# Two transformer blocks in one launch: the query root of the first attention on GpSimd, a fused negated minimum, another order at three exits, and interleaved feed-forward begins

## The reference

```
# first block
h = rmsnorm(x); z = h @ w_in                      # pool | u, v | two gates
y_a = pool_mixer(z_pool) @ w_branch_a
y_b = (gelu(u) * (tril(w_spatial) . rmsnorm(gelu(v)) + b_spatial)) @ w_branch_b
x += (sigmoid(g_a) * y_a + sigmoid(g_b) * y_b) @ w_out
x += conv_ffn(rmsnorm(x))                         # up 2 x 2816, 3-tap conv, gelu * b, down
x += sigmoid(rmsnorm(x) @ w_ple_gate) * (p @ w_ple)
x  = rmsnorm(x)
# second block, layer 0: sliding window attention; layer 1: latent attention
x += 0.5 * swiglu(rmsnorm(x)); x += attention(rmsnorm(x)); x += 0.5 * swiglu(rmsnorm(x))

def sliding_window_attention(h, ...):             # 16 heads of 64, 2 key heads, window 128
    q, k, v = split(h @ w_in)
    q, k = rmsnorm(q, q_gain), rmsnorm(k, k_gain) # over the 64 of each head
    scores = q . k / 8 + bias[bucket(distance)]   # blocks of 128 queries x 256 keys
    m = max(max(scores), sink)
    p = exp(scores - m) / (sum(exp(scores - m)) + exp(sink - m))
    return (p . v) @ w_out
```

## Time and profile before

| | |
|---|---|
| median of 3 runs | 2787.8 us (2785.0 to 2788.22) |
| profiled execution, its own time | 2790.39 us |
| its span in the profile | 2789.2 us |
| TensorE busy | 2696.5 us, 97% |
| VectorE, ScalarE, GpSimd busy | 1473.3, 972.5, 315.3 us |
| mean granted TensorE clock | 0.984 |
| chain that ended last | 86% TensorE, 8% VectorE, 4% ScalarE |

### The profile page before, as it was taken

How to read it: one execution, slowest core, us unless ns; L and a number is a source line. 1 busy time by engine, 2 the same in 40 slices (tenths; PEclk the granted TensorE clock), 3 DMA queues, 4 the chain that set the end, 5 groups by cost and what they waited for, 6 DMA issues and landing times.

```text
span 2789.2 us, 32273 instructions
## 1 busy us (share of the span) xinstructions
PE 2696.5 (97%) x13207; PEld 2260.6 (81%) x13207; DVE 1473.3 (53%) x2362; ACT 972.5 (35%) x1602; POOL 315.3 (11%) x389
## 2 busy tenths in 40 slices
PE   6899999999998999999899999999999989999999
PEld 5788788888876888888887888888888878888887
DVE  4635545655567545456675444454343677544433
ACT  3334233333354212124544222232222477432221
POOL 2000000000012000003341000010000387300000
PEclk9999999999999999999899999999999999999999
DMA  4222223623132275737222322233222200232321
GB/s 139 93 98 82 76 91 122 205 89 108 65 102 76 91 106 78 106 105 109 92 72 91 106 91 97 83 108 99 95 93 91 63 31 31 78 104 91 106 87 64
DMA packets 281194, 258.99 MB, mean 93 GB/s; under 512 B 40516, under 2 KB 276055, under 8 KB 281047
## 3 DMA queue, kind: packets, MB, share of 16 engines
q1 hardware_dynamic: 281047, 256.93, 32.0%
HBM read 242.23 MB, written 14.68 MB: 92 GB/s over the span
## 4 chain that ended last, share of the span: by engine, by line
PE 86%; DVE 8%; ACT 4%; issue 1%; POOL 0%; SPq 0%; DMA 0%; DVEq 0%; ACTq 0%; POOLq 0%
PE bank L1070 28%; PE bank L1072 27%; PE bank L1071 27%; DVE Wl L1741 1%; PE bank L1213 1%; PE bank L1081 1%; ACT Wh L1405 1%; DVE TMP L1934 1%; DVE TMP L1931 1%; DVE TMP L1810 1%; ACT TMP L1518 0%; DVE Pl L1729 0%; ACT Hh L1418 0%; PE bank L1264 0%; DVE nt L1714 0%
## 5 line engine op out<-in xcount | busy, mean ns | idle before, releaser
L1070 PE MATMUL bank<-Hh,Wl 128*128 128x512 f32 x2144 | 845.9, 395 | 15.9 <-DVE Hl L1757 15.9
L1071 PE MATMUL bank<-Hl,Wh 128*128 128x512 f32 x2144 | 838.9, 391 | 0.0
L1072 PE MATMUL bank<-Hh,Wh 128*128 128x512 f32 x2144 | 838.7, 391 | 0.0
L1405 ACT ACTIVATE Wh<-RAW 128x1024 fp32r<-128x1024 f32 (+2 forms) x454 | 441.0, 1022 | 431.8 <-PE bank L1072 391.6
L1741 DVE TENSOR_TENSOR Wl<-RAW,Wh 128x1024 fp32r<-128x1024 f32 (+2 forms) x420 | 492.6, 1216 | 170.0 <-ACT Wh L1405 169.5
L1070 PEld LDWEIGHTS bank<-Hh,Wl 128*128 128x128 f32 x2144 | 404.6, 189 | 104.2 <-issue 8.2
L1070 PE MATMUL bank<-Ph,Wl 128*128 128x512 f32 x1200 | 473.5, 395 | 13.2 <-DVE Pl L1823 3.5
L1072 PEld LDWEIGHTS bank<-Hh,Wh 128*128 128x128 f32 x2144 | 404.6, 189 | 86.2
L1071 PEld LDWEIGHTS bank<-Hl,Wh 128*128 128x128 f32 x2144 | 404.9, 189 | 85.6 <-issue 1.7
L1072 PE MATMUL bank<-Ph,Wh 128*128 128x512 f32 x1200 | 469.5, 391 | 0.0
L1071 PE MATMUL bank<-Pl,Wh 128*128 128x512 f32 x1200 | 469.3, 391 | 0.0
(11 more groups left out here) (295 smaller groups left out, 2473.1 us busy)
## 6 DMA issues: line engine op xcount, KB each, us to landing
RAW<-in_ffn_wg SPq DMA_DIRECT2D x44, 1024.0 KB, 5.2
RAW<-in_ffn_wu SPq DMA_DIRECT2D x44, 1024.0 KB, 5.1
RAW<-in_ffn_wd SPq DMA_DIRECT2D x32, 1024.0 KB, 5.2
RAW<-in_w_up SPq DMA_DIRECT2D x22, 1024.0 KB, 5.1
RAW<-in_w_in SPq DMA_DIRECT2D x20, 1024.0 KB, 5.1
RAW<-in_ffn_wd SPq DMA_DIRECT2D x16, 768.0 KB, 4.4
bias_scratch<-M SPq DMA_DIRECT2D x16, 512.0 KB, 8.1
RAW<-in_w_down SPq DMA_DIRECT2D x8, 1024.0 KB, 5.8
```

The costliest lines, as they stand in the source:

```text
L1070: mm(o, ll, rh, start=start, stop=False)
L1071: mm(o, lh, rl, start=False, stop=False)
L1072: return mm(o, lh, rh, start=False, stop=stop)
L1405: run(Wh[:, n % 3, x:y], RAW[:, n % 2, x:y], ACT.Copy).then_inc(*w_hi.up(("w_hi", n, i)))
```

## The change

- `ffn` begins with `dense_wide` for both `a` banks, then a norm step, then the `b` product with one norm step after each bank. The steps of s3's norm move from places 1 and 3 to 0 and 2.
- The first gate tile `gb` 0 is multiplied before `mix(7)`.
- Gate exit: the last `pg` bank tells after each chunk that it has been read (`frees`), and `Hh` of chunk c waits for that alone. The steps are reordered as the diff shows, with halves of chunks 0 to 2 ahead of the sums of chunk 6.
- `out_partial`: halves and sums follow one chunk behind `add_x`.
- First attention: the query root is an add and a power on GpSimd; the factor 1/8 goes into it (64 eps), and so out of the key gain. The scores are kept negated with their negated minimum, from one instruction; the exponential takes scale -1 and starts after the first half of the scores. An extra exponential on one column stands in `a_kv`.

Removed and added lines (a line "..." leaves unchanged ones out):

```diff
@@ -236,7 +236,7 @@
-    def dense(names, n, K, src, vi=0, base=0, kw=0, scaled=False, wide=False, ring=None):
+    def dense(names, n, K, src, vi=0, base=0, kw=0, scaled=False, wide=False, ring=None, frees=None):
@@ -245,7 +245,7 @@
-            do("dense", b, n, vi, K, src, ready, base, kw + c)
+            do("dense", b, n, vi, K, src, ready, base, kw + c, frees)
@@ -337,9 +337,10 @@
-                dense(ba, na, 8, "H", scaled=not begins)
+                dense(ba, na, 8, "H", scaled=not begins, wide=begins)
...
+                    norm_step()
@@ -499,6 +500,7 @@
+    gate_tile("gb", 0)
@@ -507,7 +509,7 @@
-    gated("wb", "gb", 8, branch_b)
+    gated("wb", "gb", 8, branch_b, True)
@@ -544,27 +546,41 @@
-    def gate_x(cc, b):
-        t = tmps.take(("t_pg", cc))
+    def gate_x(cc):
+        b, t = ("pg", cc // 2, cc % 2), tmps.take(("t_pg", cc))
...
+
+    def sums_x(cc):
...
-    for i in range(4):
-        n = next_tile("pg", i, 1 if i == 3 else 2)
+    for i in range(3):
+        n = next_tile("pg", i, 2)
...
-        gate_x(2 * i, ("pg", i, 0))
-        if i == 3:
-            h_new("s0")
-            for c in range(5):
-                h_pair(c, None)
-        gate_x(2 * i + 1, ("pg", i, 1))
-    for c in range(5, 8):
+        for c in range(2):
+            gate_x(2 * i + c)
+            sums_x(2 * i + c)
+    n = next_tile("pg", 3, 1)
+    dense([("pg", 3, 0)], n, 8, "H", scaled=True)
+    gate_x(6)
+    dense([("pg", 3, 1)], n, 8, "H", kw=1, frees="s0")
+    do("used", n)
+    h_new("s0")
+    for c in range(3):
...
+    sums_x(6)
+    h_pair(3, None)
+    scale([("pg", 3, 1)])
+    for c in (4, 5):
+        h_pair(c, None)
+    gate_x(7)
+    for c in (6, 7):
+        h_pair(c, None)
+    sums_x(7)
@@ -598,7 +614,7 @@
-    norm_begin("s3", "RF", (1, 3))
+    norm_begin("s3", "RF", (0, 2))
@@ -615,14 +631,14 @@
-            do("dense", b, held[j], 0, 2, src, keys(), base, c)
+            do("dense", b, held[j], 0, 2, src, keys(), base, c, None)
...
-            if j == 3:
+            for x in [c - 1] * (j == 3 and c > 0) + [c] * (j == 3 and c == 7):
...
-                    after(c)
-                if c < late:
-                    sums(c)
+                    after(x)
+                if x < late:
+                    sums(x)
@@ -924,7 +940,7 @@
-    mhalf, most = sm[:, 11:12], sm[:, 12:13]
+    mhalf, most, eps64 = sm[:, 11:12], sm[:, 12:13], sm[:, 14:15]
@@ -1012,10 +1028,10 @@
-    gk_a8 = sm[:, 10:11]
+    nsink = small[:, 48:64]
...
-    ssq, rq = small[:, 16:32], small[:, 32:48]
+    ssq, rq, rms = small[:, 16:32], small[:, 32:48], small[:, 64:80]
@@ -1112,7 +1128,7 @@
-                b, n, vi, K, src, keys, base, c = s
+                b, n, vi, K, src, keys, base, c, frees = s
@@ -1121,7 +1137,10 @@
-                ins.then_inc(*bank_full.up(b))
+                    if frees:
+                        ins.then_inc(*bank_full.up(("h_read", frees, k), *([b] if k == K - 1 else [])))
+                if not frees:
+                    ins.then_inc(*bank_full.up(b))
@@ -1412,7 +1431,7 @@
-                act.wait_ge(*maybe(("h_read", ver)))
+                act.wait_ge(*maybe(("h_read", ver, c) if ver == "s0" else ("h_read", ver)))
@@ -1559,6 +1578,8 @@
+                if half:
+                    run(sm[:, 13:14], mhalf, ACT.Exp)
@@ -1572,7 +1593,7 @@
-                run(Ph[:, g, :], bank(("a_kt", g)), ACT.Copy, scale=gk_a8).then_inc(*pair_hi.up(("a_kT_hi", g)))
+                run(Ph[:, g, :], bank(("a_kt", g)), ACT.Copy, scale=gk_a).then_inc(*pair_hi.up(("a_kT_hi", g)))
@@ -1584,9 +1605,10 @@
-                act.wait_ge(*at(("a_nmax", h)))
...
-                    run(S[:, z0:z1], S[:, z0:z1], ACT.Exp, bias=nm[:, n:n + 1], accum_out=sums_[:, n:n + 1])
+                    if n % 2 == 0:
+                        act.wait_ge(*at(("a_biased", h, n // 2)))
+                    run(S[:, z0:z1], S[:, z0:z1], ACT.Exp, bias=nm[:, n:n + 1], scale=-1.0, accum_out=sums_[:, n:n + 1])
@@ -2017,8 +2039,7 @@
-                ts(gk_a8, gk_a, 0.125, None, ALU.mult).then_inc(*dve_out.up("a_gain"))
-                dve.wait_ge(*at("a_gain"))
+                ts(nsink, sinkc, -1.0, None, ALU.mult).then_inc(*dve_out.up("a_sinks"))
@@ -2047,12 +2068,12 @@
+                if g and b == 0:
+                    dve.wait_ge(*at(("a_qss_in", g - 1)))
...
-                dve.wait_ge(*at(("a_qss", g, 3)))
-                rsqrt(rq, ssq, 64, ("a_rq", g))
@@ -2060,7 +2081,7 @@
-                stt(Pl[:, g, :], bank(("a_kt", g)), gk_a8, f(Ph[:, g, :]), ALU.mult, ALU.subtract).then_inc(
+                stt(Pl[:, g, :], bank(("a_kt", g)), gk_a, f(Ph[:, g, :]), ALU.mult, ALU.subtract).then_inc(
@@ -2072,7 +2093,8 @@
-                mx, nm = sm[:, 160 + x:164 + x], sm[:, 164 + x:168 + x]
+                nm = sm[:, 164 + x:168 + x]
+                dve.wait_ge(*at("a_sinks"))
@@ -2082,11 +2104,9 @@
-                        ins = dve.e.tensor_tensor_reduce(S[:, z0:z1], o[:, z0 - c0:z1 - c0], B[:, z0:z1], 1.0,
-                                                         sinkc[:, h:h + 1], ALU.add, ALU.max, mx[:, n:n + 1])
+                        ins = dve.e.tensor_tensor_reduce(S[:, z0:z1], o[:, z0 - c0:z1 - c0], B[:, z0:z1], -1.0,
+                                                         nsink[:, h:h + 1], ALU.add, ALU.min, nm[:, n:n + 1])
...
-                dve.wait_ge(*at(("a_biased", h, 1)))
-                ts(nm, mx, -1.0, None, ALU.mult).then_inc(*dve_out.up(("a_nmax", h)))
@@ -2228,6 +2248,7 @@
+                memset(eps64, 64 * EPS)
@@ -2282,6 +2303,16 @@
+            elif kind == "a_q_norm":
+                g, = s
+                pool.wait_ge(*at(("a_qss", g, 3)))
+                if g:
+                    pool.wait_ge(*at(("a_rq", g - 1)))
+                tt(rms, ssq, eps64.broadcast_to([128, 16]), ALU.add).then_inc(*pool_out.up(("a_qss_in", g)))
+                pool.wait_ge(*at(("a_qss_in", g)))
+                if g:
+                    pool.wait_ge(*at(("a_qn", g - 1)))
+                tt(rq, rms, mhalf.broadcast_to([128, 16]), ALU.pow).then_inc(*pool_out.up(("a_rq", g)))
```

## The result

The changed kernel takes 2753.1 us (median of 4 runs, 2752.5 to 2753.7) against 2788.0 us (2785.0 to 2789.4) for the kernel before on the same chip: ratio 0.9876, 95% interval 0.9859 to 0.9893, 34.9 us less. The forecast was 2758 us, 29.3 us less.

The account below looks back on a forecast made before the run. TensorE, busy 97% of the span, was taken as the bound, leaving only idle and low-clock time to win. Terms of 8.2, 4, 6.6, 3 and 7.5 sum to 29.3 us off 2787.8: 2758 us, range 2745 to 2774.

Parts of the forecast that it names:

- Part 1: Gate tile ahead of the last mixing product: 5.3 us of wait plus 2.9 of low clock, 8.2 us gained.
- Part 2: Gate exit into feed-forward s0: the changed order starts TensorE 3.3 us earlier; gain 4 us, bounds 0 and 8.
- Part 3: First attention, query root on GpSimd: 6.6 us from waits and 3 us from the clock.
- the waits for `M`: First attention: TensorE's waits for normalised queries shrink by 6.6 us, with VectorE's multiply held by GpSimd's split.
- The clock: First attention: less time at the low clock behind the waits, 3 us, bounds 0 and 9.5.
- no wait of TensorE goes back to the exponentials, so this is worth nothing: First attention: the fused negation and earlier exponentials gain 0; were their cover gone, 3 us.
- Part 4: First attention's exit and wide begins: 3.0 us of waits plus 4.5 of low clock, 7.5 us gained.
- The other begins: Begins of feed-forwards f, s2 and s3: no wait now, worth 0; uncovered, up to 5.4 us each.
- its sign of error: At `wb` 0, behind the last mixing product: a new TensorE wait on `Pl` would show the forecast wrong.
- GpSimd takes the gain in: Rival: multiply held by both split halves, exits' low halves alternating badly with square sums; 13 us gained, 2775 us, chance 0.10.
- the clock does not come back: Rival: waits shrink but still leave the low clock everywhere; 19 us gained, 2769 us, chance 0.15.
- the third: Rival: nothing is held and the clock stays high; 42 us gained, 2745 us, chance 0.10.

Follow-up runs that it names:

- e1: The kernel before with only the first gate tile moved ahead of the last mixing product: 2780.35 us, ratio 0.9968.
- e3: The kernel before with only the gate exit's new order and marks by row, feed-forwards still begun bank by bank: 2788.12 us, ratio 0.9994.
- e5: The kernel before with only the wide feed-forward begins: 2780.94 us, ratio 0.9970.
- e6: The changed kernel with the feed-forwards begun bank by bank again: 2756.88 us, ratio 0.9885.
- e13: The changed kernel itself, measured again in later rounds: 2756.33 us, ratio 0.9876.
- e7: The changed kernel with a separate negation on VectorE and the exponentials waiting for it, as in the kernel before: 2756.89 us, ratio 0.9885.
- e2: The kernel before with only the query root moved to GpSimd, the separate negation kept: 2776.2 us, ratio 0.9953.
- e12: The changed kernel with later query weight splits, s0's first rows ahead of the gate's seventh addition, and f begun bank by bank: 2755.63 us, ratio 0.9869.
- e10: The changed kernel without ScalarE's small early exponential that brings its table load ahead: 2757.4 us, ratio 0.9879.

## Why the prediction was right, and where it was not

**Part 1** was right in both halves, 8.2 for 8.4 (e1: 8.1 in its trace, 8.9 by the ratio). No wait for `Pl` at `wb` 0 appeared.

**Part 2** was right in its sum, 4 for 3.7, and in the step that mattered: `X` 6 held by a square sum (1.64 us for 0.69), `Hl` 0 behind it, first row 2.7 us late for the 3 forecast. Wrong was the attribution. I gave 4 us to the order and 0 to s0's wide begin; e3 shows that the order alone gives 1.4 at most, e5 the wide begin alone about 1, and the pair gives 3.7. My working had TensorE's matmuls of both banks in it, but not that the column sums between them need all eight rows and the last square sum.

**Part 3** was mis-sized: 9.6 for 14.7. By its terms: the waits for `M` gave 7.8 us (9.2 to 1.4) where 6.6 were forecast, because the third multiply was not held and the second was asked for 1.05 us later, against GpSimd's queue, than worked out. The clock gave 9.5 - 3.4 = 6.1 (the one stretch left has 6.80 us at 0.50) where I took 3 between bounds of 0 and 9.5. And 1.5 us of waits for `Pl` went (2.6 to 1.1), which I had not counted, while those for the query copies grew from 3.0 to 3.4. The size of the clock's part is that of this one trace: the clock was low for 6.8 us behind the first group here and not in e6, and 1.00 behind the second here and low for 3.4 us in e13. The step that failed in kind is "no wait of TensorE goes back to the exponentials, so this is worth nothing". It does, by way of GpSimd's queue, into which the change itself had put the root: e7 shows 1.05 us of wait; its 2.5 us in all are not told from noise. I had listed what is queued behind the root, and not what the root is queued behind once the exponentials move. e2, the root with the old exponentials, gave 12.2. And the stretched instruction of the earlier trace rows (128x16, 2.33 us for 0.17) has one input, so that of the rows I showed only the add of the earlier trace rows spoke for the multiply's being held.

**Part 4** was right, 7.5 for 8.0, and so was the chain: the low halves come every 1.70 us, each held to 1.18 or 1.19 us:

```profile
1436.77 0.68 DVE L1969 SCALAR_TENSOR_TENSOR X<-bank,X 128x512 f32<-128x512 f32 x1
1437.37 1.18 DVE L1779 SCALAR_TENSOR_TENSOR Hl<-X,P,Hh 128x512 fp32r<-128x512 f32 x1
1438.47 0.68 DVE L1969 SCALAR_TENSOR_TENSOR X<-bank,X 128x512 f32<-128x512 f32 x1
```

But either half alone gives 7 of the 8. The other begins were put at 0: f costs 0.6 us, by a wait for `Pl` in f that the forecast had not named (its sign of error was one at `wb` 0):

```profile
522.33 0.50 PE L1086 MATMUL bank<-Ph,Wl 128*128 128x512 f32 x1 [1.00 <-DVE Pl L1751]
```

It was 0.4 us before the change, and is 0.45 and 0.42 in e6 and e12, where f begins bank by bank. That the later scaling pushes the low halves behind it on VectorE is my reading of the order, not tried by itself.

**The rivals.** That GpSimd takes the gain in did not come: the multiply is held by one instruction, never by both. That the clock does not come back holds at the first group, and at s0, where the forecast had counted on nothing from it. Of the third, that nothing is held was wrong and that the clock stays high nearly right, and the time lies between its 2745 and the forecast.

## What to carry to other kernels

When work moves to another engine's queue, follow that queue in both directions: what stands ahead of the moved instruction may hang on something that had been free until then. Two edits that cure one wait don't add, and two that need each other are worth little apart, so a sum over the parts of a change is tried at its places of overlap first. At an exit with eight rows to hand over, look for the instruction that needs the last row: all that is done for the first ones ends there.

## What was not expected of the hardware

One wait, two clocks. At the first group's turn TensorE waits 1.12 us in the changed kernel and 1.12 us in e6, with the same work on all engines around it. In the first the clock is low from 1293.5 to 1300.3; in e6, by windows, it is not low at all, 3.0 us to its favour:

```profile
1290.00:1300.00 10.00, 7.75 (x62) 7.05 (x61) 7.70 (x18) 5.46 (x17) 5.30 (x4) 1.00 0.39 137
1300.00:1312.00 12.00, 11.94 (x95) 11.03 (x93) 8.63 (x23) 8.52 (x26) 9.31 (x7) 1.00 0.31 91
```

So after the same wait the clock fell in one execution and stayed in the other. What decides is open; the size of the clock's part in any one trace, 1.5 to 3 us a place, is to be taken with that doubt.

The wait at the first group changes from one execution to the next, and it follows a weight transfer. GpSimd's split of the second query tile, seen in four executions, begins when ScalarE's high half does, and that when the transfer has landed; in the changed kernel:

```profile
1272.58 2.01 ACT L1424 ACTIVATE Wh<-RAW 128x1024 fp32r<-128x1024 f32 x2 [11.53 <-DMA RAW<-in_a_w_in]
```

```profile
1273.72 4.77 POOL L2272 TENSOR_TENSOR Wl<-RAW,Wh 128x1024 fp32r<-128x1024 f32 x2 [9.16 <-ACT Wh L1424]
```

```profile
1277.21 1.31 DVE L1722 TENSOR_SCALAR nt<-sm 128x8 f32<-128x8 f32 x1
1278.56 0.17 DVE L1730 TENSOR_SCALAR nt<-nt 128x8 int32<-128x8 int32 x1
```

An instruction of VectorE on 8 elements per partition, 0.17 us when free, is held until the split ends at 1278.49, and behind it stand the keys' root, the queries' sums, GpSimd's root and the multiply:

| kernel | split ends | multiply starts | TensorE asks | its wait |
|---|---|---|---|---|
| changed | 1278.49 | 1287.33 | 1289.67 | 1.12 |
| e13 (changed) | 1279.21 | 1287.79 | 1289.38 | 1.85 |
| e10 | 1280.94 | 1289.52 | 1290.50 | 2.45 |
| e12 | 1281.51 | 1290.08 | 1290.96 | 2.55 |

In the last three the multiply starts 8.57 or 8.58 us after the split's end, in the first 8.84. So a single-input instruction of 128x8 was held, by 1.1 us, as those with two SBUF inputs are, and a transfer's landing time reaches TensorE through two other engines. Whether an earlier transfer would end this wait wasn't tried.
